# Fused groups for the Newton steps of an RWKV-7 scan: one tile's factor on the diagonal quarters, the other tile's inverse on the crosswise ones

## What is computed

```
def rwkv7_step(s, inp):
    r_t, w_t, k_t, v_t, kk_t, a_t = inp
    s_kk = jnp.einsum('bhvk,bhk->bhv', s, kk_t)
    s = s * w_t[:, :, None, :] - s_kk[..., None] * (kk_t * a_t)[:, :, None, :] + v_t[..., None] * k_t[:, :, None, :]
    o = jnp.einsum('bhvk,bhk->bhv', s, r_t)
    return s, o
...
s_final, o = lax.scan(rwkv7_step, s0.astype(f32), xs)
```

## Time and profile before

| | |
|---|---|
| three timed runs | 1619.35, 1627.39, 1629.12 us |
| median | 1627.39 us |
| the profiled execution: its time, its span | 1629.3, 1627.4 us |
| scan (all eight pairs) | 1071.6 to 1301.3 us of the span |
| granted TensorE clock, mean | 0.987 |

### The profile page before, as it was taken

One profiled execution on the slowest core, in us unless ns is written; L12 is line 12 of the kernel. 1 busy time (PEld: TensorE's weight loads), 2 busy tenths in 40 slices (PEclk: granted clock), 3 DMA queues, 4 the chain that ended last, 5 costly groups with the idle time before them and its releaser, 6 DMA issues.

```text
span 1627.4 us, 35964 instructions
## 1 busy us (share of the span) xinstructions
PE 1546.2 (95%) x14428; PEld 1146.8 (70%) x14428; DVE 958.0 (59%) x2293; ACT 642.6 (39%) x1309; POOL 82.4 (5%) x99
## 2 busy tenths in 40 slices
PE   6999999999999999999889999988998999999998
PEld 5887788878887888878655666677877854444443
DVE  5687756766466566577586676535545449333333
ACT  3255343554336541344565655542333362000001
POOL 1010000000000000000000000000000004212120
PEclk9999999999999999999999999999999999999999
DMA  6366483536544375353878675576656469999883
GB/s 230 119 209 197 155 288 123 170 114 239 195 152 149 118 260 156 105 163 126 268 253 267 183 209 168 168 242 204 215 169 192 136 267 340 367 339 353 340 326 125
DMA packets 184495, 341.71 MB, mean 210 GB/s; under 512 B 22213, under 2 KB 124101, under 8 KB 173638
## 3 DMA queue, kind: packets, MB, share of 16 engines
q1 hardware_dynamic: 167338, 256.88, 48.5%
q0 software_dynamic: 10496, 72.98, 11.9%
q10 hardware_dynamic: 6496, 9.56, 1.6%
HBM read 286.13 MB, written 55.35 MB: 210 GB/s over the span
## 4 chain that ended last, share of the span: by engine, by line
PE 81%; ACT 7%; DVE 5%; issue 3%; DMA 3%; SPq 1%; DVEq 0%; ACTq 0%
PE psum L1072 29%; PE psum L1351 24%; PE psum L1059 8%; PE psum L1045 5%; PE psum L1311 4%; PE psum L1225 3%; PE psum L1297 3%; ACT L1740 3%; DVE big L2343 2%; ACT big L1740 2%; PE psum L1656 2%; PE psum L1110 2%; PE psum L1559 1%; DMA big<-in_x_first 1%; SPq L844 1%
## 5 line engine op out<-in xcount | busy, mean ns | idle before, releaser
L1072 PE MATMUL psum<-big 128*128 128x256 f32 (+1 forms) x1920 | 436.8, 385 | 2.5 <-ACT zst L1753 2.5
L1072 PEld LDWEIGHTS psum<-big 128*128 128x128 f32 x1920 | 366.3, 191 | 60.9 <-issue 4.5
L1753 ACT ACTIVATE zst<-psum 128x256 f32<-128x256 f32 (+1 forms) x336 | 126.8, 385 | 377.0 <-PE psum L1072 370.4
L1351 PE MATMUL psum<-big 64*64 64x64 f32 (+4 forms) x5440 | 257.5, 270 | 17.3 <-issue 11.9
L1351 PEld LDWEIGHTS psum<-big 64*64 64x64 f32 (+2 forms) x5440 | 178.0, 132 | 102.7 <-issue 77.7
L1072 PE MATMUL psum<-big,wbuf 128*128 128x256 f32 (+1 forms) x768 | 180.6, 383 | 0.0
L1072 PEld LDWEIGHTS psum<-big,wbuf 128*128 128x128 f32 x768 | 145.5, 190 | 22.7 <-issue 0.4
L2343 DVE SCALAR_TENSOR_TENSOR big<-big,pars 128x512 f32<-128x512 f32 x240 | 161.0, 746 | 0.6
L1006 POOL DMA_INDIRECT big<-in_cache_v,pidx x64 | 68.4, 1069 | 640.1 <-PE psum L1311 425.9
L1740 ACT ACT_TABLE_LOAD x67 | 86.0, 1283 | 10.4 <-DMA big<-in_x_first 7.8
L1045 PE MATMUL psum<-ident,big 128*128 128x128 f32 (+3 forms) x558 | 79.4, 280 | 7.1 <-ACT big L2010 3.3
(11 more groups left out here) (327 smaller groups left out, 2039.8 us busy)
## 6 DMA issues: line engine op xcount, KB each, us to landing
big<-in_k_pages SPq DMA_DIRECT2D x432, 128.0 KB, 2.3
big<-wS SPq DMA_DIRECT2D x36, 768.0 KB, 5.8
zst<-in_k_pages SPq DMA_DIRECT2D x80, 128.0 KB, 2.7
wS<-big SPq DMA_DIRECT2D x12, 768.0 KB
wbuf<-in_w_pairs SPq DMA_DIRECT2D x18, 512.0 KB, 4.0
big<-in_w_pairs SPq DMA_DIRECT2D x18, 512.0 KB, 4.4
zT<-big ACTq DMA_DIRECT2D x16, 512.0 KB, 4.2
rwS<-big SPq DMA_DIRECT2D x32, 256.0 KB, 4.4
```

The lines of the kernel that those rows point to most:

```text
L1072: last = nc.tensor.matmul(psum[:, bank, 0:wide(p) // 2], left(k), right(k), start=first and k == 0, stop=k == 3, skip_group_check=True)
L1351: return nc.tensor.matmul(out, l, r, start=start, stop=stop, skip_group_check=True)
L1753: nc.scalar.activation(parts_[:, U % 2, COPIED_TO[j], 0:n], psum[:, (0, 1, 2, 0, 1, 2, 3)[j], 0:n], ACT.Copy, scale=0.125 if i == U_QA els ...
```

## The change

`inverse_beside_factors(s, l, l_next)` takes the place of separate groups for l = 2 to 5. It runs `inverse` of tile s at level l and `factors` of the other tile at level l_next, one product of each in turn. The products of `inverse` for l >= 2 now write to the PSUM partitions of the other chunk (crosswise quarters), and those of `factors` stay on the diagonal. So the two chunks of T change places at each level, and for odd l the factor needs I - M with its chunks exchanged, `one_f`. For that, `grams_m` computes each product a second time onto the other half of the partitions, DVE masks these two in `masked_m`, and `complement_turned` makes I - M of them. `turn(0)` waits for all four masked copies.

```
-                        gm=2, gb=4, tt0=2, sq=20, tt=20, tr=2, q=2, pcur=1, d=1, st=8, o=2, tok=6, kv=2, mt=2, x=2, o1=2)
+                        gm=4, gb=4, tt0=2, sq=20, tt=20, tr=2, q=2, pcur=1, d=1, st=8, o=2, tok=6, kv=2, mt=4, x=2, o1=2)
...
-                                    last = mm(psum[halves[c], XB[hh], x:x + CH], rin[hs, u, ALP + t, tokens(s, c)], rin[hs, u, BTI + t, tokens(s, c)])
+                                    for turned in range(2):
+                                        last = mm(psum[halves[c ^ turned], XB[hh], 256 * turned + x:256 * turned + x + CH],
+                                                  rin[hs, u, ALP + t, tokens(s, c)], rin[hs, u, BTI + t, tokens(s, c)])
...
-                        at('gm', 2)
+                        at('gm', 4)
...
+                def factor_ready(s, l, t):
+                    if t == 0 and l == 1:
                         at('gm', 2)
                         at('gb', 2 * s + 2)
+                    elif t == 0 and l in (2, 3):
+                        at('mt', 2 * (l - 2) + s + 1)
+                    if l > 1:
+                        at('tt', 4 * (l - 2) + 2 * s + t + 1)
+
+                def factor(s, l, t, hh, c):
+                    h, ct = 2 * t + hh, halves[c]
+                    left = gmx[s][ct, h, 1, :] if l == 1 else tinv[s][ct, (l - 1) % 2, h, :]
+                    right = mpow[s][ct, 0, h, :] if l == 1 else (one_f if l % 2 else one_m)[s][ct, h, :]
+                    return mm(psum[ct, G[s][t], hh * CH:(hh + 1) * CH], left, right)
...
+                def inverse_part(s, l, t, hh, c):
+                    h, ct = 2 * t + hh, halves[c]
+                    to = halves[c if l == 1 else 1 - c]
+                    return mm(psum[to, G[s][t], P + hh * CH:P + (hh + 1) * CH], factor_[s][ct, h, :], tinv[s][ct, (l - 1) % 2, h, :])
...
+                def inverse_beside_factors(s, l, l_next):
+                    for t in range(2):
+                        inverse_ready(s, l, t)
+                        factor_ready(1 - s, l_next, t)
+                        for hh in range(2):
+                            for c in range(2):
+                                one, other = inverse_part(s, l, t, hh, c), factor(1 - s, l_next, t, hh, c)
+                        one.then_inc(R['tt_mm'], 1)
+                        other.then_inc(R['sq_mm'], 1)
...
+                factors(0, 2)
                 for l in range(2, 6):
-                    factors(0, l)
-                    factors(1, l)
-                    inverse(0, l)
-                    inverse(1, l)
+                    inverse_beside_factors(0, l, l)
+                    if l < 5:
+                        inverse_beside_factors(1, l, l + 1)
+                inverse(1, 5)
...
+                    for s in range(2):
+                        v.tensor_tensor(one_f[s].rearrange("p (t b) c -> p b t c", b=2), psum[:, XB[0]:XB[1] + 1, 256 + s * P:256 + (s + 1) * P].rearrange("p b (t c) -> p b t c", t=2),
+                                        mask_m[:, :].unsqueeze(1).unsqueeze(1).to_broadcast([P, 2, 2, CH]), ALU.mult).then_inc(R['gm'], 1)
...
+                def complement_turned(s):
+                    at('gm', 2 + s + 1)
+                    v.tensor_tensor(one_f[s], id64[:, :].unsqueeze(1).to_broadcast([P, 4, CH]), one_f[s], ALU.subtract).then_inc(R['mt'], 1)
```

More of the change, by code:

```diff
@@ L445, in build @@
         one_m = (area(7424, 2, 4, CH)[:, 1], part(w_free, 0, 2, 4, CH)[:, 1])
+        one_f = (area(14656, 4, CH), area(14912, 4, CH))
         factor_ = (area(7936, 4, CH), part(w_free, 512, 4, CH))
@@ L1392, in turn @@
                     last.then_inc(R['tok_tr'], 1)
-                def factors(s, l):
-                    if l == 1:
+                def factor_ready(s, l, t):
+                    if t == 0 and l == 1:
                         at('gm', 2)
                         at('gb', 2 * s + 2)
-                    elif l == 2:
-                        at('mt', s + 1)
+                    elif t == 0 and l in (2, 3):
+                        at('mt', 2 * (l - 2) + s + 1)
+                    if l > 1:
+                        at('tt', 4 * (l - 2) + 2 * s + t + 1)
@@ new lines, in factor, with inverse_ready @@
+                def factor(s, l, t, hh, c):
[3 more added lines that the diff above has]
+                    return mm(psum[ct, G[s][t], hh * CH:(hh + 1) * CH], left, right)
+                def inverse_ready(s, l, t):
+                    if l == 1 and t == 0:
+                        at('tt0', s + 1)
+                    at('sq', 4 * (l - 1) + 2 * s + t + 1)
@@ L1400, in factors @@
+                def inverse_part(s, l, t, hh, c):
+                    h, ct = 2 * t + hh, halves[c]
+                    to = halves[c if l == 1 else 1 - c]
+                    return mm(psum[to, G[s][t], P + hh * CH:P + (hh + 1) * CH], factor_[s][ct, h, :], tinv[s][ct, (l - 1) % 2, h, :])
+                def factors(s, l):
                     for t in range(2):
-                        if l > 1:
-                            at('tt', 4 * (l - 2) + 2 * s + t + 1)
+                        factor_ready(s, l, t)
@@ L1403, in factors @@
                         for hh in range(2):
                             for c in range(2):
[L1405 to L1408, removed]
+                                last = factor(s, l, t, hh, c)
@@ L1409, in factors @@
                         last.then_inc(R['sq_mm'], 1)
                 def inverse(s, l):
-                    if l == 1:
-                        at('tt0', s + 1)
                     for t in range(2):
-                        at('sq', 4 * (l - 1) + 2 * s + t + 1)
+                        inverse_ready(s, l, t)
                         for hh in range(2):
                             for c in range(2):
-                                h, ct = 2 * t + hh, halves[c]
-                                last = mm(psum[ct, G[s][t], P + hh * CH:P + (hh + 1) * CH], factor_[s][ct, h, :], tinv[s][ct, (l - 1) % 2, h, :])
+                                last = inverse_part(s, l, t, hh, c)
@@ L2779, in rwkv_pair @@
                 complement(1)
+                complement_turned(0)
+                complement_turned(1)
                 tail(4)
```

## The result

The changed kernel takes 1649.72 us, the median of four runs (1646.05 to 1658.69). The kernel before takes 1627.59 beside it (1619.35 to 1629.12). The ratio is 1.0148, interval 1.0099 to 1.0197: 24 us slower by the ratio, 22 by the medians. The prediction was 1635.2 and within 1%. Its sign was right, its size was not, nor the 0.77 that it gave to a change of under 1%. A second comparison, on another chip with 14 runs of before, gave 1648.2 us and 1.0129 (1.0094 to 1.0165), which is 21 us.

What follows compares the result with a forecast made beforehand. TensorE, busy for 95% of the span, was taken as the bound, with fused steps held by waits between dependent halves. Per-pair costs, 8 x (0.36 + 0.47) + 7 x 0.16 = 7.8 us on 1627.4, gave 1635.2 us, range 1621 to 1650.

Steps and rivals of the forecast that it cites:

- Steps of 0.93 us: Newton levels 2 to 5 in the scan: each dependent fused step takes 0.93 us, making a pair 0.36 us longer.
- Gram products and delayed state update: Scan: doubled products in grams_m cost 0.47 us per pair; extra masked copies delay tail(1) by 0.16 in seven pairs.
- The sum of 7.8 us: Whole scan: 8 x (0.36 + 0.47) + 7 x 0.16 = 7.8 us added to 1627.4.
- the loop through ScalarE: Fused Newton step: 0.47 + 0.05 + 0.27 = 0.79 us, then a release of 0.14, making 0.93.
- the one through DVE: Fused Newton step, from product through DVE to next product: 0.47 + 0.05 + 0.29 + 0.04 = 0.85 us.
- The real gain: Rival: waits in the Newton steps are hidden, fused groups take 0.467 us each, 1609 us; chance 0.04.
- the strict order: Rival: only two MATMULs start per slot in fused halves and grams_m, step 1.16 us, 1655 us; chance 0.07.
- the stretch that the sum leaves out: Scan: 13 TensorE stops for issue, 15.4 us, read as late instructions; two are followed by half clock.
- more half-clock and later instructions: Rival: more half clock or instruction waiting in the scan adds 3 to 8 us, 1638 to 1643; chance 0.24.
- the count at 0.50 stays two: Sign to check in the scan: the number of stretches at granted clock 0.50 stays two.
- The stops swallow it: Rival: TensorE's losses ahead of a stop come off that stop in most pairs, 1627 to 1630 us; chance 0.13.
- slower by over 1%: Whole kernel slower by more than about 16 us: 0.07 strict order and 0.12 of the clock rival, 0.19.

Runs made afterwards that it cites:

- the repeat: The changed kernel measured once more against the kernel before, on another chip: 1648.2 us, 1.0129.
- split loads: Each pair load as ten DMAs of 128 KB instead of one of 1024 KB and one of 256: before 1622.78 us, changed 1634.96 us.
- small loads: Loads of pairs 2 to 7 cut to an eighth of rwS and half of rkv: before 1618.51 us, changed 1639.38, side work 1619.74, fused 1622.24.
- the side work alone: Kernel before with Gram products, masked copies and complements doubled but not read, groups kept separate and diagonal: 1633.91 us, 1.0057.
- the fused groups alone: Changed kernel without the second Gram products, masked copies and complements; odd levels take the unexchanged I - M: 1641.55 us, 1.0087.
- the key step in parts: Changed kernel with keys_values, tail(4) and the second key step in four parts moved behind fused groups: 1632.17 us, 1.0078.

## Why the prediction was wrong

**The sum was right, one of its terms by luck.** Steps of 0.93 us, +0.36 per pair, measured 0.91 and +0.35. Gram products and delayed state update, 0.47 + 0.16 = 0.63 per pair, measured 0.65. The sum of 7.8 us stands against 8 in clean pairs. That four MATMULs start per slot was right, and that the freed quarters are spent in waiting was right: the loop from product to product holds, as the 0.36 us of DVE's rest and the waits for L2781 show. But the 0.93 was the loop through ScalarE with a release of 0.14; the one through DVE I had put at 0.85. The trace has DVE's: 0.56 from a half's first product (1309.04) to DVE's instruction (1309.60), 0.29 for it, 0.07 to the next product (1309.96), 0.91 or 0.92. ScalarE is through 0.07 earlier. So the step is 0.06 longer than my sum for this loop, and the release of 0.14 that brought my figure close did not occur. The real gain and the strict order both fall. The Trainium skill ("TensorE: Matmul & The Clock Gate", Part 3) has MATMULs keep program order in start and end. What falls here is what I made of it, two per slot and 1655 us. Four starts one after the other within 0.02 us are not against the rule as such; they would be if the two MATMULs of a product stand next to each other in the program, as I had assumed, and no view shows that order.

**The failed step is the stretch that the sum leaves out.** The prediction counted the stops and the half clock of before, put nothing of them into the sum, gave "more half-clock and later instructions" 0.24 and 3 to 8 us, and wrote "the count at 0.50 stays two". Measured, what the sum left out is more than half of the loss, 13 to 16 us of 21 to 24, in three parts:

- *Half clock.* "In this trace the falls follow stops of 2 us and more" was true and too little. Before, 13 stops of up to 2.9 us brought two stretches at 0.50. In the changed kernel the stops are no longer than that (up to 2.0 us), but they stand beside the short rests of the fused steps, and the time at 0.50 grew by 26 us (24 in the repeat). I said "two to five more" stretches at 1.7 us each. It was eight stretches' worth, at 0.7 us each where they lie in the fused steps. From the scans: 16.8 us less 8 for the structure, less 3.7 for more stops (19.1 against 15.4), leaves 5 us; in the repeat (stops 14.1) 13.6 less 8, and 1.3 more for fewer stops, leaves 7. Waits too short for the view are in these too. The steps say the same by another way: 0.25 us in each 1.16 at half clock makes 5 to 6 us of 24 to 26. So with full loads the clock is the largest part of what the sum left out inside the scan, at less than half the price per us that I had given it. With small or split loads 3 to 4 us are left for it, and it is the smaller part.
- *Late instructions.* With full loads they changed by +3.7 and -1.3 us. Where the pair load is small or split, the changed kernel has 7 to 11 us more of them than before in the same form. Both parts of the change have a share: with small loads the stops are 8.5 us with the side work alone and 9.0 with the fused groups alone, where before has 2.8. For the side work a plain reason offers itself, more instructions; with 192 and 384 unread MATMULs more in the scan the stops rose further, to 25 and 26 us. Why packing the same instructions raises them is not settled. I had given this a price only inside a rival, not in the sum.
- *Ahead of the scan.* The sum has nothing there, since that code did not change. Yet in the twelve profiles with the side work (the changed kernel, its forms, the side work alone) the scan begins at 1073.4 to 1084.5 us, middle value 1075.8, and in the six without it (before and its forms, the fused groups alone) at 1070.7 to 1073.1, middle value 1071.9. The two groups do not overlap, though their edges lie close: some 4 us of the loss lie there. No run shows why.
- *The stops swallow it* (0.13) fails: only the repeat had fewer stops than the profile of before (14.1 against 15.4 us), and the step's gain that they would have had to swallow did not exist; in every other form they were more.

The same page of the Trainium skill (A second HAM failure mode) describes a clock that goes back and forth because TensorE idles briefly between groups. I had made this rule part of a rival and weighed it lightly against the row on the stops. The kernel with the fused groups alone, PEclk 0.91 with nearly unchanged stops, agrees with the rule, and so does the key step in parts, 0.99 with the waits filled. The fused groups with short stops, 0.97 to 0.99, show that here the brief rests alone did not do it.

**What stays open.** In the first comparison 24 us are lost by the ratio, 29.5 between the two profiled spans. The scan holds 16.8 of these, and 12.9 lie ahead of it (it begins at 1084.5 instead of 1071.6 us). Of the 12.9 some 4 are common to all kernels with the side work, and 5.5 are the key pages that came later; such a wait (4.3 us) came again in the side work with small loads, and in the repeat and in both kernels with fused groups alone it did not. In the repeat the scan begins 4 us later than before, of 21 lost. That these 4 us come with the side work is shown by the eighteen profiles, since ahead of the scan their code differs in nothing but how the first loads are split; whether by the place of the code in the program or in another way, no run tells.

My range, 1621 to 1650, held the time by a hair; the chance for "slower by over 1%" was 0.19 and should have been about even, since its two causes only had to add 8 us to the sum. That the time lies inside the range is luck: half of the loss has causes to which the sum gave nothing.

## What to carry to other kernels

Packing independent small products into idle quarters pays, by this case, only where the chain between dependent groups is shorter than the groups themselves. Here the loop from product through DVE to product was 0.91 us against 0.93 of work, so halving the work bought nothing. When a change thins out TensorE's work without shortening the path, price two follow-ups by name: the granted clock, and how late the instructions arrive at a queue that no longer has a lead. Where a stall has two possible causes, an experiment that takes the larger one away shows what the change does to the other.

## What was not expected of the hardware

- Short rests make stops dearer for the clock: PEclk over the scan went from 0.99 to 0.91 with the same instructions and nearly the same stops (16.6 against 15.4 us), once each step of 0.91 us held a rest of about 0.2. With the same rests and half of the stops (6.1 to 8.1 instead of 13.9 us in the Newton stretch) it stayed at 0.97 to 0.99.
- Half clock is cheap in a chain bound by another engine: a step went from 0.91 to 1.16 us, not to 1.8.
- Late instructions can be seen: every stop of over 0.8 us in the scans of before and changed ended 1.2 to 1.6 us after a packet of 16 KB on the instruction queue.
- One DMA of 1024 KB in the queues delays instructions where eight of 128 KB do not: 15.4 us of stops against 2.8 (7.7 where the eight are issued earlier). The pair load of ten pieces takes SP 5.5 us to issue, at about 0.5 us each, and comes late by it.
